# The experts' start in a two-model kernel: rows turned and gathered unscaled, the root put into the gathering matrix, the late modulation products spread singly

## What is computed

```python
h2 = rms_norm(x, norm2_g) * (1.0 + sc2) + sh2            # sh2, sc2: parts of the modulation
s = sigmoid(h2 @ router_w)                                # 16 scores a row
sel = (s + router_b).reshape(n, 4, 4)                     # 4 groups of 4 experts
best = argmax(sum(top_k(sel, 2)))                         # the group, and the best 2 in it
y = sum over the 2 experts of w_e * (silu(h2 @ w_gate[e]) * (h2 @ w_up[e])) @ w_down[e]
x = x + g2 * y                                            # g2: the last part of the modulation
```

## Time and profile before

| | us |
|---|---|
| median of 3 runs (lowest, highest) | 2092.98 (2092.33, 2095.19) |
| profiled execution, time | 2095.53 |
| profiled execution, span | 2094.2 |
| PE busy | 1973.4 (94%) |
| DVE busy | 1318.0 (63%) |
| ACT busy | 1041.0 (50%) |
| HBM read | 352.62 MB, 169 GB/s |

### The profile page before, as it was taken

The page is one execution under the profiler, slowest core; times in us unless marked ns, Lnnn a source line. Parts: engine busy times, 40 slices in busy tenths (PEclk is TensorE's granted clock), DMA queues, the critical chain, the costliest instruction groups (busy, mean ns, idle before and its releaser), DMA issues.

```text
span 2094.2 us, 29108 instructions
## 1 busy us (share of the span) xinstructions
PE 1973.4 (94%) x12289; PEld 1738.3 (83%) x12289; DVE 1318.0 (63%) x1596; ACT 1041.0 (50%) x1215; POOL 89.5 (4%) x42
## 2 busy tenths in 40 slices
PE   7799989899989999999988999999999999999998
PEld 2678888698979888899877899897799988888997
DVE  1557764577886466655697665646656575567654
ACT  2657764477764355434535433446443354555332
POOL 0390000000000000000000000000000000000000
PEclk9899999899999999999999999999999999999999
DMA  6681125398964535555530465551356555345562
GB/s 228 247 283 58 61 73 189 128 307 298 310 227 164 183 123 170 172 185 186 163 121 20 147 196 183 183 181 61 101 189 194 186 177 175 127 161 176 186 189 83
DMA packets 230059, 355.55 MB, mean 170 GB/s; under 512 B 7057, under 2 KB 179882, under 8 KB 229674
## 3 DMA queue, kind: packets, MB, share of 16 engines
q1 hardware_dynamic: 229378, 353.47, 51.3%
q10 hardware_dynamic: 552, 0.22, 0.0%
HBM read 352.62 MB, written 1.05 MB: 169 GB/s over the span
## 4 chain that ended last, share of the span: by engine, by line
PE 81%; DVE 9%; ACT 5%; DMA 3%; issue 2%; SPq 1%; POOL 0%; ACTq 0%; DVEq 0%
PE bank L573 12%; PE bank L574 12%; PE bank L575 12%; PE bank L590 11%; PE bank L591 11%; PE bank L592 11%; DVE wlo L1731 3%; ACT whi L1225 2%; PE bank L1082 2%; DVE ARENA L2325 1%; DMA raw<-in_hg_w_in 1%; PE bank L652 1%; ACT ARENA L1236 1%; PE bank L852 1%; DMA raw<-in_moe_w_gate 1%
## 5 line engine op out<-in xcount | busy, mean ns | idle before, releaser
L1731 DVE TENSOR_TENSOR wlo<-raw,whi 128x2048 fp32r<-128x2048 f32 x282 | 658.5, 2337 | 348.5 <-ACT whi L1225 348.1
L1225 ACT CAST whi<-raw 128x2048 fp32r<-128x2048 f32 x282 | 536.6, 1905 | 235.2 <-PE bank L575 210.4
L590 PE MATMUL bank<-HH,whi 128*128 128x256 f32 (+1 forms) x2048 | 605.9, 296 | 15.4 <-DVE HL L1778 9.4
L591 PE MATMUL bank<-HL,whi 128*128 128x256 f32 (+1 forms) x2048 | 597.8, 292 | 0.0
L592 PE MATMUL bank<-HH,wlo 128*128 128x256 f32 (+1 forms) x2048 | 597.5, 292 | 0.0
L590 PEld LDWEIGHTS bank<-HH,whi 128*128 128x128 f32 x2048 | 397.3, 194 | 27.8 <-issue 14.0
L591 PEld LDWEIGHTS bank<-HL,whi 128*128 128x128 f32 x2048 | 397.5, 194 | 8.9 <-issue 1.9
L592 PEld LDWEIGHTS bank<-HH,wlo 128*128 128x128 f32 x2048 | 397.0, 194 | 5.1
L573 PE MATMUL bank<-whi,YH 128*128 128x512 f32 x816 | 321.6, 394 | 10.8 <-DVE YL L2369 5.6
L574 PE MATMUL bank<-wlo,YH 128*128 128x512 f32 x816 | 319.2, 391 | 0.0
L575 PE MATMUL bank<-whi,YL 128*128 128x512 f32 x816 | 318.1, 390 | 0.0
(11 more groups left out here) (355 smaller groups left out, 1921.3 us busy)
## 6 DMA issues: line engine op xcount, KB each, us to landing
raw<-in_ffn_w SPq DMA_DIRECT2D x128, 1024.0 KB, 5.5
raw<-in_ret_w_in SPq DMA_DIRECT2D x48, 1024.0 KB, 5.2
raw<-in_hg_w_in SPq DMA_DIRECT2D x20, 1024.0 KB, 5.4
ARENA<-in_w_mod SPq DMA_DIRECT2D x16, 1024.0 KB, 7.5
raw<-in_ret_w_out SPq DMA_DIRECT2D x16, 1024.0 KB, 4.9
raw<-in_moe_w_gate SPq DMA_DIRECT2D x13, 1024.0 KB, 6.5
raw<-in_moe_w_up SPq DMA_DIRECT2D x13, 1024.0 KB, 6.9
raw<-in_moe_w_down SPq DMA_DIRECT2D x12, 1024.0 KB, 6.7
```

Source lines behind the costliest of these rows:

```text
L590: pe.matmul(ps, w[0][:, k, c], ah, start=begin, stop=False, skip_group_check=True)
L591: pe.matmul(ps, w[0][:, k, c], al, start=False, stop=False, skip_group_check=True)
L1225: ac.copy(whi[n % NS][:, :], raw[place[i]][:, :]).then_inc(*whi_("w", i))
L1731: ve.tensor_tensor(wlo[n % NS][:, :], raw[place[i]][:, :], f32(whi[n % NS][:, :]), SUB).then_inc(*wlv("w", i))
```

## The change

Eight things change, all in the experts and just ahead of them.

1. ACT and DVE have one split less ahead of `add_out` (`take(2)` becomes `take()`); it stands behind the root's chain, and the next one behind the sigmoid (ACT) or just ahead of the loop (DVE).
2. PE turns `X` itself, not the scaled `XN`; ACT and DVE copy it out of PSUM unscaled, in four copies. `XN` and its four scalings are gone, and so is the scaling and shift of `FT`.
3. The scale by column goes into the router's weights (`rws`, one DVE instruction that waits for the router's DMAs), the shift becomes eight products of `sh2` with the router's weights, and the root is applied to the 2 x 16 logits in three small instructions.
4. The gathering matrix `PG` holds the root instead of 1 (one more operand in the same instruction), and PE gathers from `X`. `PL` stays 0/1 for weights and scatter, in other memory, and is made as a whole (128 x 640).
5. The 16 late products stand singly: 1 between the transposes, 5 behind the router, 2 behind the counts, 3 behind the first weights, 5 in step 0 of the loop. They use banks 0 and 2.
6. Of the products for `CW` 2 stay ahead of the loop, 8 go into step 0, with the turn of the last block of `PL` (before, two blocks were turned there).
7. The expert group for the last block (`chosen`) is computed ahead of the loop's start by DVE, and PE waits for it ahead of its first weights product.
8. In a step of the loop the outputs, the turned `PL` and the modulation of the next block stand behind the high and low halves of the activations or behind SILU, not ahead of them.

```diff
@@ tensor_program, moe
-                def mod_late(c, half):
-                    if half == 0:
-                        banks.hold(pe, 7, "mod_rows", c)
-                    t = 2 * (c - 10) + half
-                    pe.wait_ge(s_mod[t], 64)
...
+                def mod_late(count):
+                    for n in range(state["late"], state["late"] + count):
+                        c, k = 10 + n // 8, n % 8
+                        bk = (0, 2)[c - 10]
+                        if k == 0:
+                            banks.hold(pe, bk, "mod_rows", c)
+                        if k % 4 == 0:
+                            pe.wait_ge(s_mod[n // 4], 64)
...
-                            p = PL[i][:, 128 * b:128 * b + 128]
+                            p = PG[i][:, 128 * b:128 * b + 128]
...
-                            x = pe.matmul(o, XN[i][:, c], p, start=i == 0, stop=i == 1)
+                            x = pe.matmul(o, X[i][:, c], p, start=i == 0, stop=i == 1)
...
-                mod_late(10, 0)
                 for q in range(4):
                     b = banks.hold(pe, (4, 5, 6, 1)[q], "norm", "moe", q)
-                    pe.wait_ge(*act.at("xn", q // 2))
-                    pe.wait_ge(*vec.at("xn", q // 2))
+                    pe.wait_ge(*xr.at("x", "hg", q // 2))
+                    pe.wait_ge(*xr.at("x", "hg", 2 + q // 2))
...
+                    if q == 1:
+                        mod_late(1)
...
                 pe.wait_ge(*router.all(4))
                 for k in range(8):
+                    x = pe.matmul(bank[7][:, 32:48], sh2[:, k:k + 1].to_broadcast([128, 128]), rw[:, k, :], start=k == 0,
+                                  stop=k == 7)
+                pe.wait_ge(*vec.at("rws"))
...
-                mod_late(10, 1)
+                mod_late(5)
...
-                mod_late(11, 0)
+                mod_late(2)
                 pe.wait_ge(*vec.at("places", 0))
                 gathered(0, 0, 4)
                 gathered(0, 1, 5)
-                mod_late(11, 1)
-                banks.hold(pe, 2, "weights")
-                pe.wait_ge(*vec.at("places", 1))
...
+                pe.wait_ge(*vec.at("chosen"))
+                banks.hold(pe, 3, "weights")
+                weights_of(0, 0).then_inc(*mm("weights"))
+                mod_late(3)
...
+                    if n == 0:
+                        mod_late(5)
@@ scalar_program
-                take(2)
+                take()
                 add_out("hg")
...
+                square(0)
+                square(2)
+                rows_out(0)
+                rows_out(1)
+                square(1)
+                square(3)
+                rstd("moe")
                 take()
-                ac.wait_ge(*mm.at("router"))
-                ac.activation(sg, bank[2][:, 0:32], ACT.Sigmoid).then_inc(*aps("router"))
+                ac.wait_ge(*vec.at("logits"))
+                ac.activation(sg, sg, ACT.Sigmoid).then_inc(*aps("router"))
+                take()
@@ vector_program
-                take(2)
+                take()
...
+                ve.wait_ge(*router.all(4))
+                ve.wait_ge(*vec.at("ms2"))
+                ve.tensor_tensor(rws, rw, MS[:, 16:24]..., MUL).then_inc(*vec("rws"))
+                rows_out(2)
+                rows_out(3)
                 rstd("moe", "hg")
...
+                ve.wait_ge(*mm.at("router"))
+                for i in range(2):
+                    e = slice(16 * i, 16 * i + 16)
+                    ve.tensor_scalar(sg[:, e], bank[7][:, e], ST[:, 8 + i:9 + i], None, MUL).then_inc(*vec())
+                ve.tensor_tensor(sg..., sg..., shifts, ADD).then_inc(*vec("logits"))
...
+                for i in range(2):
+                    ve.tensor_scalar(PG[i][:, 0:128], IOTA[:, 0:128], spot[:, i:i + 1], ST[:, 8 + i:9 + i], ALU.is_equal,
+                                     MUL).then_inc(*vec("places", 0))
```

More of the change, by code:

```diff
@@ L559, in tensor_program @@
         def tensor_program(pe):
-            state = {"next": 0}
+            state = {"next": 0, "late": 0}
             def take():
@@ L857, in places @@
                     banks.hold(pe, 3, "places", r)
-                    for b in range(2 * r, min(2 * r + 2, 5)):
+                    for b in PLACES[r]:
                         for i in range(2):
@@ L861, in places, with weights_of @@
                                              PL[i][:, 128 * b:128 * b + 128], ident)
+                    if r == 0:
+                        for b in range(1, 5):
+                            x = weights_of(b, 256 + 4 * b)
                     x.then_inc(*trn("places", r))
+                def weights_of(b, o):
+                    for i in range(2):
+                        x = pe.matmul(bank[3][:, o:o + 4], PL[i][:, 128 * b:128 * b + 128], cwt[:, 4 * i:4 * i + 4],
+                                      start=i == 0, stop=i == 1)
+                    return x
                 def hidden(n, up):
@@ L1484, in moe @@
                         ac.activation(AG[n % 2], bank[6 + n % 2][:, 0:256], ACT.Silu).then_inc(*aps("moe", n))
+                    if n in (1, 4, 5):
+                        r = (1, 4, 5).index(n)
+                        ac.wait_ge(*trn.at("places", r))
+                        for y in PLACES[r]:
+                            ac.copy(PT[y], bank[3][:, 256 * (y % 2):256 * (y % 2) + 256]).then_inc(*aps("places", r))
+                        if r:
+                            banks.free(("places", r), aps)
+                    if n % 4 in (2, 3) and b < 4:
+                        modulated(b + 1, n % 4 - 2)
+                        high(b + 1, n % 4 - 2)
+                    if n == 1:
+                        mod_rows(11)
                     if n:
@@ L2105, in moe @@
                 ve.wait_ge(*aps.at("router"))
-                ve.wait_ge(*router.all(4))
                 bias = RB.rearrange("p (i e) -> p i e", i=1).to_broadcast([128, 2, 16])
@@ new lines, in moe @@
+                for i in range(2):
+                    ve.tensor_scalar(PG[i][:, 0:128], IOTA[:, 0:128], spot[:, i:i + 1], ST[:, 8 + i:9 + i], ALU.is_equal,
+                                     MUL).then_inc(*vec("places", 0))
+                own(ve.tensor_tensor(wts, rk, sg, MUL))
+                own(ve.tensor_reduce(den, halves(wts), AX, ADD))
+                own(ve.reciprocal(den, den))
+                own(ve.tensor_tensor(halves(wts), halves(wts),
+                                     den.rearrange("p (i e) -> p i e", e=1).to_broadcast([128, 2, 16]), MUL))
@@ new lines, in moe @@
+                own(ve.tensor_reduce(quads(cwt), wts.rearrange("p (i g j) -> p i j g", i=2, g=4), AX, ADD))
+                for i in range(2):
+                    ve.tensor_scalar(PL[i], IOTA, spot[:, i:i + 1], None, ALU.is_equal).then_inc(*vec())
+                own(ve.tensor_scalar(tot[0:1, :], bank[3][0:1, 8:12], 128.5, None, ALU.is_ge))
+                own(ve.tensor_tensor(tot[0:1, :], tot[0:1, :], GROW[0:1, 0:4], MUL))
+                own(ve.tensor_reduce(den[0:1, 0:1], tot[0:1, :], AX, ADD))
@@ L2142, in moe @@
+                ve.tensor_scalar(GI[0:1, 0:1], den[0:1, 0:1], 1.0 / 128, None, MUL).then_inc(*vec("chosen"))
+                banks.free(("counts",), vec)
+                for i in range(2):
+                    ve.tensor_scalar(PG[i][:, 128:640], IOTA[:, 128:640], spot[:, i:i + 1], ST[:, 8 + i:9 + i],
+                                     ALU.is_equal, MUL).then_inc(*vec("places", 1))
                 ve.wait_ge(*mm.at("gather", 0, 1))
@@ L2186, in moe @@
                         banks.free(("hidden", n), vps)
+                    if n == 1:
+                        ve.wait_ge(*aps.at("places", 0))
+                        ve.tensor_copy(CW[:, 4:20], bank[3][:, 260:276]).then_inc(*vps("weights"))
+                        banks.free(("places", 0), vps)
+                        ve.wait_ge(*vps.last())
+                    if n % 4 in (2, 3) and b < 4:
+                        low(b + 1, n % 4 - 2)
                     if n:
```

129 lines of the change are left out of this document (47 added, 82 removed).

## The result

| | before | changed |
|---|---|---|
| median beside each other, us (lowest, highest; 9 runs each) | 2095.03 (2089.73, 2097.65) | 2087.9 (2085.72, 2090.62) |
| profiled execution: time, span | 2095.53, 2094.2 | 2090.62, 2089.0 |
| PE / DVE / ACT busy | 1973.4 / 1318.0 / 1041.0 | 1972.5 / 1313.9 / 1036.7 |

The ratio is 0.9971, 95% interval [0.9962, 0.998]: by it the changed kernel is 6.1 us faster, 4.2 to 8.0; the two medians lie 7.1 apart. The forecast was 3.9 us less and 2089.1. The profile is of the slowest of the nine executions.

What follows compares the result with a forecast made beforehand. The tensor engine was taken to bound the kernel, standing or at half clock in the 38.8 us before the first expert. 7.2 - 6.3 + 1.7 + 1.3 = 3.9 us, from median 2092.98 to 2089.1; range 2083 to 2093.5.

Steps and rivals of the forecast that it cites:

- The additions: Behind the output projection: without the split ahead, DVE's four additions to X end at 366.0, 5.6 us earlier.
- The new wait: Ahead of the shift products: PE stands 2.7 us for the router's small loads, the last landing at 369.8.
- L: Rival: the router's loads land late, at 372.5, with 2.7 us more standing; gain 1.2, time 2091.8 us; chance 0.18.
- Shift and router: Eight shift and sixteen router products on PE run at half clock, 10.3 us, ending at 380.1.
- The clock's return: Behind the router: five late products take 4.4 us at full clock plus 1.5 while the clock comes back.
- Counts to the first expert: From the counts at 386.0 through the gather, the first expert starts at 396.0, 7.2 us earlier.
- Work moved into step 0: Eight narrow and five late products move into the loop's step 0 on PE, costing 6.3 us there.
- Clock at the first expert: Wide products now stand ahead of the first expert, so the clock's fall there goes: 1.7 us gained, at least 0.
- The loop's order: In the experts' loop: 3.8 us of old PE waits go, 2.5 come new, 1.3 gained; bounds +3.8 and -7.4.
- S: Rival: the loop loses, PE waiting for late splits at eight steps; at 1.4 us each 2097.8 us; chance 0.09.
- W: Rival: the clock stays up in the router, first expert at 390.8, gain 9.1, time 2083.9 us; chance 0.15.

Runs made afterwards that it cites:

- split_back: Changed kernel with the second split put back ahead of the additions to X on ACT and DVE: 2095.74 us, ratio 1.0006 to the kernel before.
- rw_alone: Changed kernel with the router's weights on their own semaphore, so shift products and scaled weights wait for those 64 KB only: 2084.77 us, ratio 0.9957.
- before_again: The kernel before, run and profiled again without any edit: 2094.48 us, ratio 1.0003.
- loop_new: Kernel before with only the changed kernel's new order inside a step of the experts' loop: 2091.38 us, ratio 0.9982.
- narrow_back: Changed kernel with all ten narrow products for the places' weights ahead of the loop again, none in step 0: 2088.28 us, ratio 0.9971.
- fill_gap: Changed kernel with three of the five late products behind the router moved ahead of the shift products: 2088.12 us, ratio 0.9972.
- rw_fill: rw_alone with one more late product ahead of the shift, three instead of five behind the router, six in step 0: 2084.71 us, ratio 0.9957.
- after_again: The changed kernel, run and profiled again without any edit: 2088.73 us, ratio 0.9975 to the kernel before.
- loop_old: Changed kernel with the old order inside a loop step, outputs and next block's modulation and halves ahead of the first split: 2092.39 us, ratio 0.9993.
- split_loop: Kernel before with two edits only, those of split_only and loop_new together: 2084.72 us, ratio 0.9946.
- split_only: Kernel before with only the second split moved from ahead of add_out to behind FT: 2088.18 us, ratio 0.9966.
- split_best: split_loop with the second of the two splits behind the sigmoid on ACT and behind the places' comparisons on DVE: 2079.68 us, ratio 0.9932.

## Why the prediction was right, and where it was not

The interval of the ratio lies on the faster side and the time in the range, 1.2 us below the forecast. That it is so near is in part luck. The gain was forecast as 3.9 us, below the whole interval of 4.2 to 8.0; by the medians it is 7.1, 3.2 more. But the forecast set out from 2092.98, and beside the changed kernel the kernel before took 2095.03, 2.05 more. The two misses leave 1.2. Taken by its own steps, with both profiles of the changed kernel and the times counted from the end of the projection:

- **The additions.** Right: done 1.6 us behind the projection's end, as the forecast had it (366.0 against 364.4). split_back shows the chain of reasons, and prices the split at the whole gain.
- **The new wait.** Right: the load landed 6.0 and 5.8 us behind the projection (forecast 5.4), and PE stood 3.04 and 2.79 (forecast 2.7). rw_alone takes it away. L (later landing) didn't come about. The 2.0 us of fixed part that the Trainium skill gives (DMA: Bandwidth & Descriptors, "Anatomy of one DMA — SWDGE (gpsimd) path"), for another path of issue, would have put it ahead of the transposes' end. For the constants it gives 3.0 us with 1.0 of movement, an estimate; all runs show 5.6 to 6.2. The 64 KB of the router's weights come near it, 2.2 us, in the four runs with late additions (before, before_again, split_back, loop_new); in the ten with early ones, right behind a load of 1 MB, they took 4.2 to 6.0.
- **Shift and router.** The size was right in the first profile (10.3 forecast, 10.3 measured from 368.56 to 378.89) and 2 us too long in the second (8.3). The reason given, "PE has stood nearly 3 us behind short transposes", fits two runs only: in the first profile and in narrow_back the clock fell while PE stood. It isn't needed: rw_alone and fill_gap fall with gaps of 0.68 and 0.36 and rw_fill with none, and after_again and loop_old run the shift at full clock behind 2.79 and 2.70. What the runs have in common is the longer stretch of narrow products, 48 records: the clock was down before their end in all eight runs that have the shift; with 32, behind wide products and a gap of 0.26, it did not fall in the three runs of the kernel before with the split moved. That the shift products themselves bring it was not tried alone.
- **The clock's return.** Mis-sized: 1.5 us were added to the five late products; it was 3.0 (7.36) and 2.1 (6.52).
- **Counts to the first expert.** Right: 10.0 forecast, 10.1 measured (386.18 to 396.3). The start came out as 33.8 and 30.7, with 31.6 forecast.
- **Work moved into step 0.** Right: 210.5 to 204.27 in split_loop is 6.2 to 6.3.
- **Clock at the first expert.** The size was right: 208.88 to 207.28 in split_only, 1.6, forecast 1.7. The lower bound, a fall in step 0 by the moved products, didn't come. The reason isn't shown: the forecast put the fall down to L965 straight ahead, and split_only, loop_new, split_loop and split_best keep it there and have no fall. What decides it stays open.
- **The loop's order.** The term that was most off: +1.3 forecast, 3.0 measured from either side (loop_old, loop_new). The new waits were as forecast, 1.7; the further 0.8 for late activations didn't come, and the five old waits cost 0.9 more than the 3.8 us of standing that the forecast took them for, as PE's busy time shows. S is refuted for this order: PE waited for no split in the loop.

So the sum, 7.2 - 6.3 + 1.7 + 1.3, was in the two profiles 5.0 and 7.9 - 6.3 + 1.6 + 3.0: 3.3 against before and 6.2 against before_again. The middle two of its four terms were near; the first varied by 3 us with the moment of the clock's fall, and the last was less than half of what was measured. **W** was half there, in the second profile: the clock up in the shift, not in the router.

What the forecast didn't ask is what each part of the change is worth beside its simplest. Start and loop together hold all of the work in either kernel: 244.34 and 241.17 in the two profiles of the changed one, 237.32 in split_loop. Unscaled rows, root in the gathering matrix, shift products, single late products and the other places of the splits together cost 4 to 7 us there, 5 to 6 by the ratios (0.9971 and 0.9975 to 0.9946), and hardly anything with the wait taken away (rw_alone, 237.44; by the ratio up to 2 us, within the intervals). What they remove, the root and the scaling ahead of the transposes, had cover in the late products as soon as the additions were early. It stays open which of them costs how much.

## What to carry to other kernels

When an engine stands behind a chain, first look for an instruction in the chain that belongs to other work (here a split that waited for a cast that waited for a load), and move that alone; only then see what is still late, for algebra that takes other steps off the path may add a wait and work where the cover was free. Price a change of order by the length of the whole stretch in both kernels, busy time and standing together: here the waits alone gave 2.1 us of 3.0. Put moved work where its own engine's wait is longest in the trace, on each engine apart.

## What the hardware showed that was not expected

The granted clock fell in the midst of narrow products with PE busy throughout: in rw_alone 4.2 us after the first of them, behind a gap of only 0.68 us, and in rw_fill 4.8 us after, behind none. The same kernel differed in the moment of the fall from one execution to the next, by which its start took 33.8 or 30.7 us. It came back 2.5 us after the wide late products behind the router had begun in before and before_again, 5.0 us after in loop_new, and 3.5 to 5.9 us after in the kernels with the shift. In split_best PE stood 1.91 us ahead of the counts and the clock stayed at 1.00; in split_only and split_loop, after 4.03 and 4.23 us, it fell (0.57 over 382 to 386). The length of the gap alone does not settle it, for in fill_gap it had come back just ahead of a wait of 1.38 us and fell again 2 us behind it (0.79 over 384 to 386). And the 64 KB of the router's weights took 2.2 us from issue to landing with no large load ahead, 4.2 to 4.5 behind one of 1 MB, and 5.9 to 6.0 there in the two kernels that count them on a semaphore of their own; the 388 KB of constants took 5.6 to 5.7 and 5.9 to 6.2.
